# Sample attention of a two-layer encoder: rows of (head, token) by keys, a running sum on VectorE, value products 32 columns at a time

## What is computed

```python
# stick-breaking: 8 heads of 64
z = einsum('bqhd,bkhd->bhqk', q, k) * scale
log_fail = where(earlier, log_sigmoid(-z), 0.0)            # earlier: key before query
between = cumsum(log_fail, axis=3, reverse=True) - log_fail
w = where(earlier, exp(log_sigmoid(z) + between), 0.0)
out = einsum('bhqk,bkhd->bqhd', w, v)

# differential: 4 heads, components c = 0, 1
s = einsum('bqhcd,bkhcd->bhcqk', q, k) * scale
pr = softmax(where(visible, s, -inf), axis=-1)
w = pr[:, :, 0] - lam * pr[:, :, 1]
out = einsum('bhqk,bkhe->bqhe', w, v)
```

## Time and profile before

| what | value |
|---|---|
| three runs | 3218.28, 3223.35, 3228.25 us; median 3223.35 |
| the profiled execution, its own time | 3217.51 us |
| its span, first to last instruction | 3215.7 us |
| TensorE busy over the span | 92% |
| mean granted TensorE clock | 0.947 of 2.4 GHz |

### The profile page before, as it was taken

How to read it: one execution, slowest core, us unless ns; L and a number is a source line. 1 busy time by engine, 2 the same in 40 slices (tenths; PEclk the granted TensorE clock), 3 DMA queues, 4 the chain that set the end, 5 groups by cost and what they waited for, 6 DMA issues and landing times.

```text
span 3215.7 us, 43928 instructions
## 1 busy us (share of the span) xinstructions
PE 2971.9 (92%) x16841; PEld 2608.1 (81%) x16841; DVE 837.8 (26%) x1824; ACT 944.4 (29%) x1984; POOL 965.4 (30%) x888
## 2 busy tenths in 40 slices
PE   7999998989878899999789999988788989999988
PEld 7989987865767799899669989976645879989976
DVE  3111123124242411111442111133344332111143
ACT  3211223234242421221342212233344333212233
POOL 4432423320000442343334324332100034324323
PEclk9999998989787899999899999989799999999999
DMA  4322312320221231232113212222100013213212
GB/s 124 95 69 66 90 54 62 109 92 21 85 66 42 77 96 55 81 92 78 55 45 105 76 59 88 69 61 74 41 1 25 19 56 104 79 56 95 77 40 92
DMA packets 256073, 222.67 MB, mean 69 GB/s; under 512 B 15168, under 2 KB 200896, under 8 KB 255952
## 3 DMA queue, kind: packets, MB, share of 16 engines
q1 hardware_dynamic: 253120, 211.07, 21.5%
q10 hardware_dynamic: 2304, 8.39, 0.7%
q0 software_dynamic: 528, 1.64, 0.2%
HBM read 212.44 MB, written 8.60 MB: 69 GB/s over the span
## 4 chain that ended last, share of the span: by engine, by line
PE 80%; DVE 9%; ACT 3%; DMA 3%; POOL 3%; issue 3%; SPq 0%; ACTq 0%; DVEq 0%; POOLq 0%
PE ps L1554 22%; PE ps L1555 22%; PE ps L1556 22%; PE ps L1765 3%; PE ps L1739 2%; PE ps L1657 2%; DVE y_rows L1235 2%; DVE x_rows L1238 2%; DVE xt_lo L1253 1%; PE ps L1675 1%; PE ps L1684 1%; ACT silu_gate L762 1%; DVE y_rows L1247 1%; PE ps L1753 1%; POOL rs L1090 1%
## 5 line engine op out<-in xcount | busy, mean ns | idle before, releaser
L1554 PE MATMUL ps<-xt_hi,gu_hi 128*128 128x256 f32 (+1 forms) x2816 | 875.1, 311 | 24.0 <-DVE xt_lo L1253 18.2
L1555 PE MATMUL ps<-xt_lo,gu_hi 128*128 128x256 f32 (+1 forms) x2816 | 873.2, 310 | 0.0
L1556 PE MATMUL ps<-xt_hi,gu_lo 128*128 128x256 f32 (+1 forms) x2816 | 872.9, 310 | 0.0
L1076 POOL TENSOR_TENSOR ch_lo<-ch_raw,ch_hi 128x512 fp32r<-128x512 f32 (+2 forms) x324 | 403.6, 1264 | 1065.6 <-ACT ch_hi L724 1065.4
L1071 POOL TENSOR_TENSOR gu_lo<-gu_raw,gu_hi 128x512 fp32r<-128x512 f32 x352 | 455.4, 1297 | 728.4 <-ACT gu_hi L720 727.7
L1554 PEld LDWEIGHTS ps<-xt_hi,gu_hi 128*128 128x128 f32 x2816 | 537.4, 191 | 29.1 <-issue 17.5
L1555 PEld LDWEIGHTS ps<-xt_lo,gu_hi 128*128 128x128 f32 x2816 | 537.6, 191 | 0.0
L1556 PEld LDWEIGHTS ps<-xt_hi,gu_lo 128*128 128x128 f32 x2816 | 537.4, 191 | 0.0
L720 ACT ACTIVATE gu_hi<-gu_raw 128x512 fp32r<-128x512 f32 x352 | 222.7, 633 | 649.5 <-DMA gu_raw<-in_ffn_gu 649.1
L724 ACT ACTIVATE ch_hi<-ch_raw 128x512 fp32r<-128x512 f32 (+2 forms) x324 | 197.9, 620 | 563.4 <-DMA ch_raw<-in_ffn_dn 343.7
L1554 PE MATMUL ps<-ch_hi,ht_hi 128*128 128x512 f32 x880 | 343.4, 390 | 0.0
(11 more groups left out here) (224 smaller groups left out, 3070.9 us busy)
## 6 DMA issues: line engine op xcount, KB each, us to landing
gu_raw<-in_ffn_gu SPq DMA_DIRECT2D x352, 256.0 KB, 3.0
ch_raw<-in_ffn_dn SPq DMA_DIRECT2D x176, 256.0 KB, 3.4
ch_raw<-in_ab_in SPq DMA_DIRECT2D x48, 256.0 KB, 2.8
ch_raw<-in_ple_gate SPq DMA_DIRECT2D x32, 256.0 KB, 3.9
g_pre<-in_norms ACTq DMA_DIRECT2D x8, 512.0 KB, 4.9
g_post<-in_norms ACTq DMA_DIRECT2D x8, 512.0 KB, 3.9
ch_raw<-in_ab_out SPq DMA_DIRECT2D x16, 256.0 KB, 3.1
k_raw<-in_cache_sb_k SPq DMA_DIRECT2D x8, 512.0 KB, 3.8
```

What stands on the lines that cost most here:

```text
L1076: pool.tensor_tensor(ch_lo[:, c, 0:p["n"]], ch_raw[:, c, 0:p["n"]], ch_hi[:, c, 0:p["n"]].bitcast(F32), ALU.subtract).then_inc(ch_lo_ok, c ...
L1554: pe.matmul(out, a[0], b[0], start=start, stop=False)
L1555: pe.matmul(out, a[0], b[1], start=False, stop=False)
L1556: return pe.matmul(out, a[1], b[0], start=False, stop=stop)
```

## The change

The samples leave the two pipelines and get one of their own, `cache_scores` and `caches_pe`, `caches_act`, `caches_dve`, used for both attentions, each with 8 units. Rows are (head, token) or (head, component, token) on 128 partitions, 384 keys as columns, the scores being written by four groups of 32 rows as the differential part had them. For stick-breaking the sum over later keys is a `tensor_tensor_scan` on VectorE from the last key to the first, and the mask is added to the scores as a product with `z_sel`. Three transposes bring the weights to keys on partitions; the value products have 32 columns of weights and 128 columns of values, four of them (j fixed) beside each other on 32 partitions each. A row product with `merge` at the end picks the rows of each head and adds components. The stick pipeline keeps 32 prompt units; the keys of the first samples are transposed in its last rounds, and in the last round of the pairs.

```diff
             def stick_act(units, sample):
...
-                    for u in units[m + 3:m + 4]:
-                        if u["prep"]:
-                            copy_kt(u["prep"])
+                    if m == L - 2:
+                        copy_kt(sample[0]["prep"])
...
+            def caches_act(units):
...
+                def softplus(u):
+                    a = ca_e[:, u["par"]]
+                    act.wait_ge(ca_min, u["b"] + 1)
+                    act.activation(a, a, ACT.Exp).then_inc(ca_exp, 1)
+                    act.wait_ge(ca_exp, u["b"] + 1)
+                    act.activation(a, a, ACT.Ln, bias=one[:]).then_inc(ca_ln, 1)
...
+                soft_kind = units[0]["kind"] == "soft"
+                if soft_kind:
+                    copy_kt(units[0]["prep"])
+                copy_kt(units[1]["prep"])
+                (soft_weights if soft_kind else softplus)(units[0])
+                for n in range(L + 1):
+                    if n >= 1:
+                        u = units[n - 1]
+                        act.wait_ge(ca_t, u["i"] + 1)
+                        if u["i"] >= 2:
+                            act.wait_ge(ca_o, u["i"] - 1)
+                        act.activation(ca_wt[:, u["par"]], PS[:, 3, 0:PAST + P], ACT.Copy).then_inc(ca_cp, 1)
+                    if n + 2 < L:
+                        copy_kt(units[n + 2]["prep"])
+                    if n + 1 < L:
+                        (soft_weights if soft_kind else softplus)(units[n + 1])
+                    if n < L and not soft_kind:
+                        stick_weights(units[n])
...
+            def caches_dve(units):
...
+                def rows(u):
...
+                        dve.wait_ge(ca_o, u["i"] + 1)
+                        dve.tensor_tensor(out.rearrange("p (c d) -> p c d", c=2), src.rearrange("p (c d) -> p c d", c=2),
+                                          consts[:, a:a + 2].unsqueeze(2).to_broadcast([P, 2, HD]), ALU.mult).then_inc(ca_row, 1)
...
+                def summed_up(u):
...
+                    dve.tensor_tensor(sp, z, ca_e[:, u["par"]], ALU.max).then_inc(ca_max, 1)
+                    dve.wait_ge(ca_max, u["i"] + 1)
+                    dve.tensor_tensor_scan(ca_sum[:, u["par"], ::-1], sp[:, ::-1], sp[:, ::-1], 0.0, ALU.add, ALU.max
+                                           ).then_inc(ca_scan, 1)
+
+                def exponents(u):
...
+                    dve.tensor_tensor(ca_w[:, u["par"]], PS[:, S_BANK[u["par"]], 0:PAST + P], ca_sum[:, u["par"]], ALU.subtract
+                                      ).then_inc(ca_diff, 1)
...
+                for n in range(L + 2):
+                    if n >= 2:
+                        rows(units[n - 2])
+                    if n < L and not soft_kind:
+                        summed_up(units[n])
+                    if n + 1 < L:
+                        (maximum if soft_kind else clamped_scores)(units[n + 1])
+                    if n < L and not soft_kind:
+                        exponents(units[n])
+                dve.wait_ge(ca_pv, units[-1]["i"] + 1)
+                evict_group(units[-1])
...
+                    dve.tensor_copy(z_sel.rearrange("p (h t) -> p h t", h=SB_HEADS), ident[:, 0:DEC_T].unsqueeze(1).to_broadcast(
+                        [P, SB_HEADS, DEC_T])).then_inc(z_ok, 1)
+                    dve.tensor_copy(z_win[:], const("batch_win")).then_inc(z_ok, 1)
+                    stick_dve(stick[st["stick0"]:st["stick1"]], st["stick_units"])
+                    caches_dve(st["stick_units"])
...
+            def cache_scores(u):
...
+                for h in range(4):
+                    pe.matmul(out[32 * h:32 * h + 32, 0:PAST], q[:, h], kt[:, u["par"], h, :], start=True, stop=True,
+                              skip_group_check=True)
+                for h in range(4):
+                    pe.matmul(out[32 * h:32 * h + 32, PAST:PAST + P], q[:, h], u["k"][:, h, PROMPT:TOK], start=False, stop=True,
+                              skip_group_check=True)
+                if u["kind"] == "stick":
+                    at = P - DEC_T - u["b"] * DEC_T
+                    mm = pe.matmul(out[:, PAST:PAST + P], z_sel[:], z_win[:, at:at + P], start=False, stop=True, skip_group_check=True)
...
+            def caches_pe(units):
+
+                L = len(units)
+                for n in range(L + 2):
+                    if 1 <= n <= L:
+                        u = units[n - 1]
+                        pe.wait_ge(ca_wts, u["i"] + 1)
+                        if u["i"] >= 1:
+                            pe.wait_ge(ca_cp, u["i"])
+                        for j in range(3):
+                            mm = pe.transpose(PS[:, 3, j * P:(j + 1) * P], ca_w[:, u["par"], j * P:(j + 1) * P], ident[:])
+                        mm.then_inc(ca_t, 1)
+                    if n + 2 < L:
+                        transpose_keys(units[n + 2]["prep"])
+                    if n + 1 < L:
+                        cache_scores(units[n + 1])
+                    if 1 <= n <= L:
+                        u = units[n - 1]
+                        pe.wait_ge(ca_cp, u["i"] + 1)
+                        if u["i"] >= 1:
+                            pe.wait_ge(ca_row, u["i"])
+                        pe.wait_ge(vraw_in[u["par"]], 16 * (u["i"] // 2 + 1))
+                        for j in range(3):
+                            val = v_raw[:, u["par"], j, :] if j < 2 else u["v"][:, PT, :]
+                            for h in range(4):
+                                mm = pe.matmul(PS[32 * h:32 * h + 32, 0, 0:P],
+                                               ca_wt[:, u["par"], j * P + 32 * h:j * P + 32 * h + 32], val[:, h * P:(h + 1) * P],
+                                               start=j == 0, stop=True, skip_group_check=True)
+                        mm.then_inc(ca_o, 1)
+                    if n >= 2:
+                        u = units[n - 2]
+                        out = bank_of(u)[:, 0:HALF].rearrange("p (h n) -> p h n", h=4)
+                        pe.wait_ge(ca_row, u["i"] + 1)
+                        pe.matmul(out[:, :, u["b"] * DEC_T:(u["b"] + 1) * DEC_T], ca_rows[:, u["par"]],
+                                  const("merge").rearrange("p (h t) -> p h t", h=4), start=True, stop=True,
+                                  skip_group_check=True).then_inc(ca_pv, 1)
+
+            def stick_pe(units, sample):
...
+                    if n == L - 3:
+                        transpose_keys(sample[0]["prep"])
+                    if n == L:
+                        transpose_keys(sample[1]["prep"])
+                    if n == L + 2:
+                        cache_scores(sample[0])
...
-            def pair_pe():
+            def pair_pe(sample):
...
+                    if n == L + 1:
+                        transpose_keys(sample[0]["prep"])
```

More of the change, by code:

```diff
@@ L100, in const_table @@
     put("diag", k < q)
-    put("batch_tri", (k // DEC_T == q // DEC_T) & (k % DEC_T < q % DEC_T))
+    m = np.arange(BATCH_WIN)[None, :] - (P - DEC_T)
+    put("batch_win", np.where((m >= 0) & (m < k), 0.0, -BIG))
     cos, sin = rope_table(DF_ROT, ROPE_THETA)
@@ L293, in encoder @@
                              "pair_pv"))
+        z_ok = sem("z_ok")
+        ca_z, ca_min, ca_exp, ca_ln, ca_max, ca_scan, ca_diff, ca_wts, ca_t, ca_cp, ca_o, ca_r, ca_row, ca_pv = (
+            sem("ca_" + n) for n in ("z", "min", "exp", "ln", "max", "scan", "diff", "wts", "t", "cp", "o", "r", "row", "pv"))
         sub_sq, sub_mm, sub_ln, sub_rs, sub_ok = (sem("sub_" + n) for n in ("sq", "mm", "ln", "rs", "ok"))
@@ L394, in prep_bank @@
         def prep_bank(pr, b):
-            return (1, 2)[b] if pr["kind"] == "stick" else (0, 3)[b]
+            return (1, 2)[b] if pr["kind"] in ("stick", "soft") else (0, 3)[b]
         stick = []
@@ L406, in new_group, with caches @@
             return groups[-1]
+        def caches(st, kind, g, name):
+            st[kind + "_units"] = []
+            for b in range(DEC_B):
+                i = len(preps)
+                preps.append({"i": i, "k": io[f"cache_{name}_k"][0, b], "v": io[f"cache_{name}_v"][0, b], "kind": kind})
+                st[kind + "_units"].append({"i": i, "par": i % 2, "b": b, "kind": kind, "prep": preps[-1], "g": g, "first": b == 0,
+                                            "q": qbd[name + "_q"], "k": QKV[name + "_k"], "v": QKV[name + "_v"]})
         mixers = [st for st in stages if st["kind"] in ("ab", "mla")]
@@ L528, in encoder @@
                 u["i"] = n
-                u["w"] = DF_HEADS * DEC_T if u["prep"] and u["prep"]["kind"] == "soft" else P
                 if u["last"]:
@@ L560, in keys_done @@
         def keys_done(pr):
-            return (sb_z if pr["kind"] == "stick" else at_s), pr["last"] + 1
+            return (ca_z, pr["i"] + 1) if pr["kind"] in ("stick", "soft") else (at_s, pr["last"] + 1)
         def unit_done(pr):
-            return (sb_pv if pr["kind"] == "stick" else at_pv), pr["last"] + 1
+            return ca_o, pr["i"] + 1
```

(10 more changed lines are left out.)

178 lines of the change are left out of this document (91 added, 87 removed).

## The result

The changed kernel takes 3149.18 us (median of 4 runs, 3144.88 to 3152.63) where the kernel before takes 3222.4 (4 runs, 3218.28 to 3228.25): a ratio of 0.9771, with a 95% interval from 0.975 to 0.9791.

The account below looks back on a forecast made before the run. TensorE's instructions, by number not columns, were taken to pace the sample parts; 40.7 + 26.2 - 0.6 = 66 us, less a clock deduction 59, so 3158.5 profiled and 3164 us median, range 3150 to 3175.

Parts of the forecast that it names:

- Stick samples, 40.7 us: Stick-breaking sample part: fill, 4.8 us loop and drain let the pairs begin at 836.0 instead of 876.7, 40.7 us earlier.
- The table copies, 0.6 us: VectorE ahead of the first clamp at 700.41: two copies for the mask tables, hidden by nothing, lose 0.6 us.
- Differential samples, 26.2 us: Differential sample part: TensorE sets a 4.15 us loop, ending at 974.8 instead of 1001.0, 26.2 us earlier.
- the 0.4 of idle for the changes of weight size: TensorE's cost per unit: two more changes between 32-column and full-width weights, each with 0.20 us of idle.
- The deduction for the clock, 7.4 us: Both sample parts: granted clock 0.9, a fifth of the time at the low level, cutting the gain from 66 to 59.
- The offset of 5.85 us: Whole kernel: median of the runs lies 5.85 us above the profiled execution, turning 3158.5 into 3164 us.
- The low end of the range: Whole kernel: 3150 us, with full clock throughout and 0.7 us for the value products.
- The low clock throughout: Rival: clock stays low in both sample parts, gain 29 us, 3194 us; chance 0.24.
- Products not beside each other: Rival: 32-column value products don't run beside each other, 2.73 us instead of 1.08, 3183 us; chance 0.07.
- The loads: Rival: key and value loads landing one after the other make the loops 7.8 us, gain 14, 3209 us; chance 0.05.
- The slow scan: Rival: VectorE's scan per stick sample costs beyond 2.35 us; at 12 us the kernel is 18 us slower, 3241; chance 0.03.

Follow-up runs that it names:

- casts_early: Against the changed kernel, only the two mask-table copies on VectorE moved to right behind the lam reduction; 3141.44 us, ratio 0.9751.
- late fills: Against the changed kernel, GpSimd's two fills of the padded queries held back until VectorE's sixth clamp, copies left in place; 3148.24 us, ratio 0.9769.

## Why the forecast held in kind and was too small

The forecast of a gain of 59 us in the profiled execution met 70.3. Step by step:

- **Stick samples, 40.7 us.** The structure was right: fill, a loop of 4.8 us (4.73) set by the chain and not by TensorE, ScalarE's 3.2 us beside it, a scan that costs nothing until 2.35 us. The filling came as forecast, 6.57 us from the first sample's scores (799.80) to the end of the weights' Exp (805.86 + 0.51), against 6.7. The stretch was still 3.6 us too long. The first sample's scores came 11.8 us behind the last prompt scores, for 11. The first round ran in part at the low clock (granted 0.73) and took 6.35 us, so that the five rounds were 1.3 longer than 5 x 4.8. The last two rounds and the drain took 1.7 longer (granted 0.64 from 835.5 to 842 us).
- **The table copies, 0.6 us.** This is a step that failed, in the other direction. "Nothing hides them there: 0.6 us lost" took two short copies by themselves and forgot GpSimd, whose fill the trace of before has at 700.17, beside the very place. They hold the first clamp for 2 us, and the kernels with them are 7.7 us slower in the median; the profiles put most of what is beyond the 2 us down to the clock. With them out of the way the stretch from the prompt scores to the pairs is 141.0 us (694.90 to 835.91 in casts_early), within 2 us of the 142.7 forecast without them. In the first profile of the changed kernel this miss cannot be seen: from the first to the last prompt scores it took 92.9 us, for 92.4 before and 93.0 forecast. That is luck. The profile of the kernel before was itself slow there: the same prompt code took 88.4 us in the kernel with the old stick samples and the new differential ones.
- **Differential samples, 26.2 us.** This is a term that was mis-sized: too small by 4.1. TensorE sets the loop as said, but it is 3.41 us instead of 4.15. The value products cost 0.80 for 1.08 and the scores 1.04 for 1.16, and the 0.4 of idle for the changes of weight size was counted on top of groups whose slots already hold it. Waits for keys came to 2.1 us at the start (1.5 forecast) and for the last values to 1.2.
- **The deduction for the clock, 7.4 us.** This is the step that failed most. It carried the prompt parts' 0.9 over to both new loops. Of the 7.4 us, 4.2 (a fifth of 26.2 - 5) stood for the differential part, which was granted 0.99. The stick part was granted 0.92, near the 0.9, but what the low clock cost there, in the first round and the drain, is already counted in the 3.6 us above.
- **The offset of 5.85 us** from the profiled execution to the median. It was that of one execution of the kernel before; for the changed kernel it is 1.9. The part of the program behind the last eviction took 5.2 us less than before without having changed; over the profiles of the changed kernel and its variants it lies between 2210 and 2220 us, so this, too, is how one execution differs from another.

Added up: 7.4 + 4.1 + 5.2 less 1.7 for the late start of the mixer and 3.6 for the stick part, are 11.4 us (70.3 - 59, to rounding), and 3.9 more by the offset. The low end of the range assumed a full clock and 0.7 for the value products and still lay 0.8 us too high, since the idle that was counted on top, the offset of one execution and the unchanged rest of the program were in it.

The rivals. The low clock throughout: refuted in both loops. Products not beside each other: refuted, the 24 take 0.79 us and not the 2.73 of that rival; in the worse order they take 1.51. The loads: 217 GB/s were reached, with the 3.3 us of waits above. The slow scan: 0.96 us, 1.4 short of mattering. The prediction had taken 0.8. The Trainium skill, DVE: opcode table, instruction layouts, handler registers and perf-mode slots, section Datapath and trigger behaviour, gives the scan half throughput, which made an estimate of 1.1; the run lies between. The Trainium skill, TensorEngine Tiling (Array Packing), section Theoretical Speedup, gives up to a factor of four, which made an estimate of 0.68 for the value products; the trace says 0.79 to 0.80, nearer to that than to the 1.08 from the score rows.

## What to carry to other kernels

Here products of few columns cost by the instruction: the 24 value instructions of a differential sample took 2.73 us with 16 columns each and 0.80 with 128, and the two stages shrank from 91.0 to 54.0 and from 65.0 to 34.2 us. The order in which the four groups take turns was worth a factor of 1.9 in the value products by itself. Before placing even a short copy on VectorE ahead of a chain's first step, look at what GpSimd runs at that moment; the trace of before shows it. A delay on a chain that feeds TensorE is to be priced with the clock that it may cost later, and not by its own length alone. One profile of a kernel is not its median: the two profiles of the changed kernel differ by 5.9 us in the prompt part.

## What the runs showed that was not expected

- Copies of 0.22 and 0.28 us took 1.90 us beside two fills of GpSimd, and both ended with them.
- A delay of 2 us at the start of the prompt units went with 7.7 to 9.8 us of the time and with a granted clock of 0.54 to 0.89 in place of 1.00 some 70 us later; with late fills the clock fell to 0.69 there with 0.5 us of delay.
- The same 24 value products took 0.79 us with the four groups in turn and 1.51 us with the six instructions of one group in a row.
- Three more scans per sample cost the loop 1.48 us of their 2.97, and one more cost it nothing.
